# Adding the experts' rows to the residual by scatters with addition instead of gathering them in a closing stage

## What is computed

```
h   = h + moe(rmsnorm(h, ffn_norm))
# moe: each row picks one of 4 groups and 2 of the 4 experts in it; 16 experts, FF = 256
for e in range(16):
    he = silu(t @ w1[e]) * (t @ w3[e])
    y  = y + gates[:, e:e+1] * (he @ w2[e])
y_prompt, y_sample = rmsnorm(h[meta rows dropped], final_norm)
```

## Time and profile before

| | us |
|---|---|
| median of 3 runs (1346.1 to 1353.96) | 1346.58 |
| the profiled execution | 1341.16 |
| its span, first to last instruction | 1339.4 |
| busy in the span: PE / DVE / ACT / POOL | 1141.3 / 718.1 / 506.5 / 310.0 |

### The profile page before, as it was taken

One profiled execution on the slowest core, in us unless ns is written; L12 is line 12 of the kernel. 1 busy time (PEld: TensorE's weight loads), 2 busy tenths in 40 slices (PEclk: granted clock), 3 DMA queues, 4 the chain that ended last, 5 costly groups with the idle time before them and its releaser, 6 DMA issues.

```text
span 1339.4 us, 18555 instructions
## 1 busy us (share of the span) xinstructions
PE 1141.3 (85%) x5999; PEld 926.0 (69%) x5999; DVE 718.1 (54%) x1328; ACT 506.5 (38%) x909; POOL 310.0 (23%) x274
## 2 busy tenths in 40 slices
PE   4999999989898989989899999965988989899800
PEld 3888899934776777777787776854776767777600
DVE  3430510155645554545454553447777777788646
ACT  3334221133212222122223232305767777777611
POOL 2100400000000000000000000004665666666454
PEclk9999999999878988898999999976999999999965
DMA  6340141180101011110101010006778876673287
GB/s 241 108 146 0 56 131 50 48 252 19 32 17 52 32 64 37 43 63 17 63 17 63 17 48 9 32 32 199 266 263 277 277 271 230 240 246 130 79 324 256
DMA packets 93987, 158.93 MB, mean 119 GB/s; under 512 B 13712, under 2 KB 62304, under 8 KB 93920
## 3 DMA queue, kind: packets, MB, share of 16 engines
q1 hardware_dynamic: 81152, 113.49, 25.0%
q0 software_dynamic: 11680, 42.47, 9.2%
q10 hardware_dynamic: 1088, 2.10, 0.4%
HBM read 167.81 MB, written 40.55 MB: 156 GB/s over the span
## 4 chain that ended last, share of the span: by engine, by line
PE 57%; DVE 12%; DMA 10%; issue 9%; ACT 6%; SPq 2%; POOL 2%; POOLq 0%; ACTq 0%; DVEq 0%
PE ps L918 10%; DMA below<-in_w 7%; PE ps L885 5%; PE ps L755 4%; PE ps L773 4%; DVE low L1603 4%; PE ps L1926 4%; PE ps L1928 4%; PE ps L1927 4%; PE ps L844 3%; PE ps L1921 2%; PE ps L1920 2%; PE ps L1922 2%; SPq L1211 2%; ACT high L1318 2%
## 5 line engine op out<-in xcount | busy, mean ns | idle before, releaser
L1603 DVE TENSOR_TENSOR low<-below,high 128x1024 fp32r<-128x1024 f32 x128 | 198.2, 1595 | 70.0 <-ACT high L1318 62.6
L1784 POOL TENSOR_SCALAR arena<-arena 128x1 f32<-128x1 f32 (+5 forms) x38 | 14.8, 390 | 728.4 <-ACT arena L743 325.9
L1279 POOL TENSOR_TENSOR low<-below,high 128x1024 fp32r<-128x1024 f32 x64 | 148.5, 2340 | 106.3 <-ACT high L1339 106.3
L1416 PE MATMUL ps<-high 128*128 128x512 f32 x384 | 158.5, 413 | 16.1 <-DVE low L1613 11.4
L1418 PE MATMUL ps<-high,low 128*128 128x512 f32 x384 | 152.9, 398 | 0.0
L1417 PE MATMUL ps<-low,high 128*128 128x512 f32 x384 | 152.7, 398 | 0.0
L1318 ACT ACTIVATE high<-below 128x1024 fp32r<-128x1024 f32 x128 | 128.9, 1052 | 44.9 <-DMA below<-in_w 44.9
L553 ACT ACTIVATE arena<-ps 128x512 f32<-128x512 f32 (+7 forms) x109 | 56.9, 531 | 232.0 <-PE ps L755 231.6
L918 PE MATMUL ps<-arena 128*128 128x256 f32 (+1 forms) x576 | 133.3, 385 | 3.3 <-ACT arena L553 2.8
L918 PEld LDWEIGHTS ps<-arena 128*128 128x128 f32 (+1 forms) x576 | 107.1, 188 | 29.3 <-issue 6.7
L755 PE MATMUL ps<-arena 128*128 128x128 f32 (+4 forms) x613 | 100.3, 290 | 7.0 <-ACT arena L735 2.5
(11 more groups left out here) (215 smaller groups left out, 1988.4 us busy)
## 6 DMA issues: line engine op xcount, KB each, us to landing
below<-in_w SPq DMA_DIRECT2D x256, 256.0 KB
below<-in_w POOLq DMA_DIRECT2D x64, 512.0 KB
y_dram<-arena SPq DMA_DIRECT2D x32, 512.0 KB, 3.0
arena<-in_x_prompt SPq DMA_DIRECT2D x16, 512.0 KB
below<-in_w_in SPq DMA_DIRECT2D x12, 512.0 KB, 6.8
out<-arena SPq DMA_DIRECT2D x9, 512.0 KB, 6.7
arena<-in_w_o SPq DMA_DIRECT2D x1, 4096.0 KB, 16.6
h_dram<-arena SPq DMA_DIRECT2D x8, 512.0 KB, 2.6
```

The costliest lines, as they stand in the source:

```text
L1279: pool.tensor_tensor(w2_lo[s % UN][:, c], w2_in[:, c], w2_hi[s % UN][:, c].bitcast(F32), ALU.subtract).then_inc(s_w2lo, 1)
L1416: pe.matmul(out, x_hi, w_hi, start=start, stop=False)
L1603: dve.tensor_tensor(chunk(w13_lo[j], c), chunk(w13_in, c), chunk(w13_hi[j], c).bitcast(F32), ALU.subtract).then_inc(s_w13lo, 1)
```

## The change

The expert rows are no longer stored in `y_dram` and gathered. Instead POOL adds the 128 rows of each slot straight to the residual rows in `h1_dram` by an indirect DMA with addition, one after the other: two slots may hold the same row, so each waits for the landing of the one before. An empty place must not add to row 0; it is sent to one of 128 spare rows behind the T real ones, each place to its own. The spare rows are filled once by a DRAM to DRAM copy in the attention phase.

The gate has to be in the row before it is added, so it is multiplied into the gated product. For that a gate and a row number are needed for each place of a slot: `slot_gate` and `row_i`. They come from a second product on PE with `pos_at`: its other side, `more_at`, holds an indicator of occupied places and the gate in three bfloat16 parts, so that their sum is the float32 gate.

The closing stage loads all nine tiles of sums, squares, scales and stores them from the same buffer.

```diff
     # routing, after the gates
+        left = gates.rearrange("p k t -> p (k t)")
+        for n in range(3):
+            link(dve.tensor_copy(gate_part[:, n, :], left))
+            if n < 2:
+                link(dve.tensor_tensor(gate_rest[:, n, :], left, gate_part[:, n, :], ALU.subtract))
+                left = gate_rest[:, n, :]
...
-        dve.tensor_copy(slot_i, slot.rearrange("p (k t) -> p k t", k=2)).then_inc(s_slots, 1)
...
     # PE, between the product for tok_i and the turn of slot 0
+        pe.wait_ge(s_more, 4)
+        for k in range(2):
+            for t in range(NT):
+                n = k * NT + t
+                ins = pe.matmul(ps[:, 5, 0:4 * SLOT_TILES], pos_at[0:MOE_ROWS[t], n, :], more_at[0:MOE_ROWS[t], n, :],
+                                start=n == 0, stop=n == 2 * NT - 1)
+        ins.then_inc(s_moreps, 1)
...
     # DVE, before the loop
         split_weights(0, 0)
+        dve.tensor_copy(more_at[:, :, 0:SLOT_TILES], is_tile).then_inc(s_more, 1)
+        for n in range(3):
+            dve.tensor_tensor(more_at[:, :, (n + 1) * SLOT_TILES:(n + 2) * SLOT_TILES], is_tile,
+                              gate_part[:, n, :].unsqueeze(2).to_broadcast([P, 2 * NT, SLOT_TILES]),
+                              ALU.mult).then_inc(s_more, 1)
         dve.wait_ge(s_mx, 1)
         turned(0)
+        dve.wait_ge(s_moreps, 1)
+        held, far = ps[:, 5, 0:SLOT_TILES], row_f[:, 2, :]
+        dve.tensor_reduce(slot_gate, ps[:, 5, SLOT_TILES:4 * SLOT_TILES].rearrange("p (k s) -> p s k", k=3), AX.X, ALU.add)
+        link(dve.tensor_scalar(row_f[:, 0, :], held, -1.0, 1.0, ALU.mult, ALU.add))
+        link(dve.tensor_scalar(far, row_f[:, 0, :], tab[:, C_TOK:C_TOK + 1], float(T), ALU.mult, ALU.add))
+        link(dve.tensor_tensor(row_f[:, 1, :], far, row_f[:, 0, :], ALU.mult))
+        link(dve.tensor_tensor(row_f[:, 1, :], row_f[:, 1, :], rt[:, 23, 0:SLOT_TILES], ALU.add))
+        dve.tensor_copy(row_i, row_f[:, 1, :]).then_inc(s_rowi, 1)
...
     # DVE, in every slot
+            link_gate(s, j)      # gate_now[:, j] = slot_gate[:, s], then a wait for it
-            dve.tensor_tensor(g_row, act_h, ps[:, 3 + j, FF:2 * FF], ALU.mult).then_inc(s_mg, 1)
+            dve.scalar_tensor_tensor(out=g_row, in0=act_h, scalar=gate_now[:, j:j + 1], in1=ps[:, 3 + j, FF:2 * FF],
+                                     op0=ALU.mult, op1=ALU.mult).then_inc(s_mg, 1)
...
     # SP: no stores of y in the loop and none after it
     # SP, attention phase
+        sp.dma_start(h1_dram[T:T + P, :], x_prompt[0, 0:P, :]).then_inc(s_spare, 16)
     # POOL
+        def scatter(s):
+            if s == 0:
+                pool.wait_ge(s_rowi, 1)
+                pool.wait_ge(s_h1st, 16 * NT)
+                pool.wait_ge(s_spare, 16)
+            else:
+                pool.wait_ge(s_yst[(s - 1) % UN], 16 * ((s - 1) // UN + 1))
+            pool.wait_ge(s_mya, s + 1)
+            pool.wait_ge(s_myv, s + 1)
+            pool.indirect_dma_start(
+                out=h1_dram, out_offset=bass.IndirectOffsetOnAxis(ap=row_i[:, s:s + 1], axis=0),
+                in_=y_row[:, s % UN, :], in_offset=None, compute_op=ALU.add).then_inc(s_yst[s % UN], 16)
...
             if s + UN < SLOT_TILES:
                 gather(s + UN)
+            if s >= 2:
+                scatter(s - 2)
+        for s in range(SLOT_TILES - 2, SLOT_TILES):
+            scatter(s)
...
     # closing stage, SP
+        for j in range(UN):
+            sp.wait_ge(s_yst[j], 16 * uses(j))
         for t in range(NT):
             R = MOE_ROWS[t]
+            sp.dma_start(res[0:R, t, :], h1_dram[t * P:t * P + R, :]).then_inc(s_res[t], 16)
     # POOL: no fetch, rsqrt_mean alone. ACT squares res[t] when it has landed. DVE, for each tile:
+            dve.scalar_tensor_tensor(out=x, in0=x, scalar=y_stat[0:R, 1, t:t + 1], in1=fin_b[0:R, :], op0=ALU.mult,
+                                     op1=ALU.mult).then_inc(s_yo, 1)
```

More of the change, by code:

```diff
@@ L245, in hybrid_layer @@
     gates = r.take(2, NT)
-    slot_i = r.take(2, NT).bitcast(I32)
+    row_i = r.take(SLOT_TILES).bitcast(I32)
+    slot_gate = r.take(SLOT_TILES)
+    gate_now = r.take(2)
     tok_i = r.take(SLOT_TILES).bitcast(I32)
@@ L252, in hybrid_layer @@
     spread = Region(r.at)
-    is_tile = spread.take(2 * NT, SLOT_TILES)
     spread.at = (spread.at + 1) // 2 * 2
     tok_at = spread.take(2 * NT, SLOT_TILES).bitcast(BF16)
-    pos_at = spread.take(2 * NT, P // 2).bitcast(BF16)
     at_least = spread.take(2 * NT, SLOT_TILES)
@@ L270, in hybrid_layer @@
     (xg_hi, xg_lo), (g_hi, g_lo) = ([q.take(*dims) for q in (hi, lo)] for dims in ((KC, P), (2, P)))
-    r = Region(keep.at + 8000)
[L273 to L277, removed]
+    late = Region(below_floats + hi.at)
+    is_tile = late.take(2 * NT, SLOT_TILES)
+    pos_at = late.take(2 * NT, P // 2).bitcast(BF16)
+    more_at = late.take(2 * NT, 2 * SLOT_TILES).bitcast(BF16)
+    gate_rest = late.take(2, 2 * NT)
+    gate_part = late.take(3, NT).bitcast(BF16)
+    row_f = late.take(3, SLOT_TILES)
+    assert late.at <= below_floats + parts_floats
+    r = Region(keep.at + 8000)
+    res = r.take(NT, D)
     fin_b = r.take(D)
@@ L280, in hybrid_layer @@
     y_stat = r.take(2, NT)
-    h1_dram = nc.dram_tensor("h1_dram", [T, D], F32).ap()
+    h1_dram = nc.dram_tensor("h1_dram", [T + P, D], F32).ap()
     hn_dram = nc.dram_tensor("hn_dram", [T, D], F32).ap()
@@ L287, in hybrid_layer @@
     f_dram = nc.dram_tensor("f_dram", [P, HH, T], F32).ap()
-    y_dram = nc.dram_tensor("y_dram", [SLOTS, D], F32).ap()
     phase_end = sem("phase_end")
@@ L1126, in hybrid_layer @@
     s_rank = sem("s_rank")
-    s_slots = sem("s_slots")
+    s_spare = sem("s_spare")
+    s_gate = sem("s_gate")
+    s_more = sem("s_more")
+    s_moreps = sem("s_moreps")
+    s_rowi = sem("s_rowi")
     s_etab = sem("s_etab")
@@ L1153, in hybrid_layer @@
     s_fin_w = sem("s_fin_w")
-    s_res = [sem(f"s_res{i}") for i in range(FB)]
-    s_yab = [sem(f"s_yab{i}") for i in range(FB)]
-    s_comb = sem("s_comb")
+    s_res = [sem(f"s_res{i}") for i in range(NT)]
     s_ysq = sem("s_ysq")
@@ L1159, in hybrid_layer @@
     s_yo = sem("s_yo")
-    s_yout = [sem(f"s_yout{i}") for i in range(FB)]
+    s_yout = sem("s_yout")
     UN = 2
@@ L1212, in body @@
                                  cond=new).then_inc(s_w13in[c], 16)
[L1213 to L1220, removed]
         expert_turns(sp, body)
-        for s in range(SLOT_TILES - 3, SLOT_TILES):
-            store_y(s)
-            sp.dma_start(y_dram[s * P:(s + 1) * P, :], y_row[:, s % UN, :]).then_inc(s_yst[s % UN], 16)
         sp.wait_ge(phase_end, 12)
         sp.dma_start(fin_b, final_norm.rearrange("(a n) -> a n", a=1).to_broadcast([P, D])).then_inc(s_fin_w, 16)
[L1230 to L1238, removed]
+        for j in range(UN):
+            sp.wait_ge(s_yst[j], 16 * uses(j))
         for t in range(NT):
             R = MOE_ROWS[t]
+            sp.dma_start(res[0:R, t, :], h1_dram[t * P:t * P + R, :]).then_inc(s_res[t], 16)
+        for t in range(NT):
             sp.wait_ge(s_yo, t + 1)
             if t < 8:
-                sp.dma_start(y_prompt[0, t * P:(t + 1) * P, :], y_out[:, t % FB, :]).then_inc(s_yout[t % FB], 16)
+                sp.dma_start(y_prompt[0, t * P:(t + 1) * P, :], res[:, t, :]).then_inc(s_yout, 16)
             else:
[L1245 to L1249, removed]
+                sp.dma_start(y_sample[0], res[0:SAMPLE, t, :]).then_inc(s_yout, 16)
+        sp.wait_ge(s_yout, 16 * NT)
     def moe_pool(pool, rsqrt_mean):
@@ L1303, in moe_pool @@
             rsqrt_mean(y_stat[0:R, 1, t:t + 1], y_stat[0:R, 0, t:t + 1], D, s_ysq, s_yrs, t + 1)
-            if t + FB < NT:
-                fetch(t + FB)
     def moe_act(act):
@@ L1375, in moe_act @@
             R = MOE_ROWS[t]
-            act.wait_ge(s_comb, t + 1)
+            act.wait_ge(s_res[t], 16)
             if t:
                 act.wait_ge(s_ysq, t)
-            act.activation(y_sq[0:R], res[0:R, t % FB, :], ACT.Square,
+            act.activation(y_sq[0:R], res[0:R, t, :], ACT.Square,
                            accum_out=y_stat[0:R, 0, t:t + 1]).then_inc(s_ysq, 1)
@@ L1620, in moe_dve, with link_gate @@
         split_weights(0, 0)
+        dve.tensor_copy(more_at[:, :, 0:SLOT_TILES], is_tile).then_inc(s_more, 1)
[3 more added lines that the diff above has]
+                              ALU.mult).then_inc(s_more, 1)
         dve.wait_ge(s_mx, 1)
         turned(0)
+        dve.wait_ge(s_moreps, 1)
[6 more added lines that the diff above has]
+        dve.tensor_copy(row_i, row_f[:, 1, :]).then_inc(s_rowi, 1)
+        def link_gate(s, j):
+            dve.tensor_copy(gate_now[:, j:j + 1], slot_gate[:, bass.ds(s, 1)]).then_inc(s_gate, 1)
+            dve.wait_ge(s_gate, s + 1)
         def body(it, j, first, last):
@@ L1652, in moe_dve @@
         dve.wait_ge(s_fin_w, 16)
-        def finish(t):
+        for t in range(NT):
             R = MOE_ROWS[t]
```

(3 more changed lines are left out.)

## The result

| | before | after |
|---|---|---|
| median, us | 1347.15 (1346.1 to 1353.96) | 1362.32 (1360.43 to 1371.1) |
| profiled execution | 1341.16 | 1360.43 |
| its span | 1339.4 | 1358.7 |

The ratio is 1.012, 95% interval 1.0084 to 1.0155: the changed kernel is slower by 1.2%. Two later rounds on other chips gave 1.0145 (1.0106 to 1.0184) and 1.0113 (1.0072 to 1.0155). The forecast was 1353.6; its own range was 1340 to 1360, and the range over all rivals 1326 to 1382.

A forecast was written before the change was run, and what follows sets the result against it. Bound: a DVE-PE-ACT ring per slot, DMA slightly late for new experts, and a byte-moving closing stage. Terms -25 +4 +4 +24 = +7 us gave 1348 profiled, 1353.6 median; range 1340 to 1360, with rivals 1326 to 1382.

The forecast's parts named there:

- The sum: Whole change: -25 closing stage, +4 start, +4 gate copy, +24 scatters in the loop, together +7 us.
- the three stretches: Router's first operation to first turn of rows, loop to last y copy, closing stage: forecast +4, +28 and -25 us.
- Part 1: Closing stage: gathers, multiply-adds and y_dram traffic go, three serial scatters and nine loads remain; 25 us gained, bounds 7 to 34.
- the cadence: Closing stage: time per tile at the slowest station for the eight tiles after the first, taken as 2.1 us.
- Part 2: Start, before the first turn of rows: more gate operations and PE's second routing product delay it, +4 us, bounds 1 and 6.
- the linked operations: Start, ahead of the routing: five more gate operations in a chain, +1.0 us, minus 0.1 for a removed copy.
- Part 3: Loop, DVE: the gate copy before the gated product adds 0.2 us per turn, +4 us in all, bounds 2.5 and 10.
- the ring: Loop, slot with its expert loaded: DVE splits, gated product, PE turn, ACT splits, DVE's next splits; period 10.61 us.
- Part 4: Loop: scatter traffic beside the last weight chunks costs 1.6 us per new expert, 15 times, +24 us, bounds 5 and 38.
- A: Rival, loop: scatter traffic hides in idle DMA time, load term 0 to 6 instead of 24, 1330 to 1336 us; chance 0.3.
- B: Rival, loop: scatter landings over 10.6 us set the period; at 12 us +43, total 1382 us; chance 0.13.
- C: Rival, loop: weight loads lose the full double price, 2.5 us each, +38 instead of 24, 1368 us; chance 0.22.

The follow-up runs named there:

- the repaired kernel: Changed kernel with gate copied a slot ahead, gate parts and second product after the first turn, no POOL drain, roots in five groups: 1348.75 us, ratio to before 1.0016.
- plain scatters: Changed kernel with scatters that overwrite full rows instead of adding: 1351.31 us, ratio to before 1.0016.
- thin ones: Changed kernel with scatters that do not add and write only the first 64 of 1024 columns, to a narrow tensor of their own: 1327.42 us, one execution.
- b_store_mid: Kernel before, with SP's store of y of slot s-3 moved from after the fourth weight chunk to after the second: 1357.09 us, ratio 1.0072.
- after_again: The changed kernel once more, unchanged, on another chip: 1366.73 us, ratio to before 1.0145.

## Why the prediction came out as it did

**Sign and size.** The sum was +7 on the three stretches and they gave +10.2; the time is 8.7 us over the forecast, 2.3 over its own range of 1340 to 1360 and inside the wide one. Within 1% was held likelier (0.38) than slower (0.34); it came out just beyond. The good sum is in part luck: the closing stage gave 4.5 us less than forecast and the loop grew by 2.1 less.

**Part 1, closing stage, -25 forecast, -20.5 measured.** L (a scatter's time from issue to landing) was taken as 6, and the last ones follow each other at 6.1 to 6.3; scatter 29 was put 8.4 us ahead of y 31's arrival and came 8.5; the cadence was taken as 2.1 and is 2.00, with POOL's operation at 1.28 us beside DVE's. The term that failed is one that is not in the sum: POOL's drain. It was read from nothing, because in before it lay hidden behind the last slots, and it held the loads back 4.3 us, shown by the repaired kernel. The first load also landed in 5.3 us instead of 4.1.

**Part 2, start, +4 forecast, +4.8 measured.** From the router's first operation to DVE's weight splits it is 1.3 us longer, where 0.9 were forecast for the linked operations; the product took 2.44 us instead of 2.0. Moving the gate parts and the product out of the way brought 26.1 back, which shows that this stretch was all theirs.

**Part 3, gate, +4 forecast.** 0.2 us in the ring was 0.18 and another 0.07 for the product, which had been put at 0. Shown are five free slots instead of eight, 1.3 us; in the slots with loads the term stays open.

**Part 4, scatters, +24 forecast, 21.7 measured** (after less the kernel without them, one execution each), 1.4 per new expert against 1.6. The mechanism is the one forecast, traffic beside the last weight chunk. The chunks on the chain between 957 and 1215 us took 5.0 to 8.6 us in before, 9.1 to 12.3 in after, 8.6 to 10.0 with plain scatters, 5.1 to 8.4 without scatters and 5.4 to 8.0 with thin ones, and the loop is long or short with them. POOL's issues and the waits for landings are excluded as causes; bytes and packets were not parted. The working was right for a partly wrong reason: it took its bounds from the addition (1.3 us plain, 2.5 double) and chose low. In fact plain scatters already cost about 16 us (20 against the thin ones), 1.1 to 1.4 per expert and so the full plain price, and the addition, though it about doubles a row's engine time, adds 0.4 to 0.9 each.

**The rule on the shared engines.** The Trainium skill (DMA: Bandwidth & Descriptors, Issuing engines are not separate DMA queues) says that transfers from all issuing engines run on the same 16 DMA engines and interleave. This case's runs agree: plain scatters from POOL's queue made SP's weight chunks land later, 8.6 to 10.0 us against 5.1 to 8.4 without them. Stores behind the weights in SP's own queue cost nothing that can be read: the loop of before is 356.5 us with them, and the loops without full rows of y are 360.7 and 356.3.

**The rivals.** A (it hides) is refuted: ACT's wait for weights rose from 29.1 to 32.0 us to between 47.6 and 53.2, as the forecast had it (some 50). B (the landing becomes the ring) is too: landings were 5.8, 8.0 and at most 10.9 us under periods of 10.8 and more, and POOL waited for them 1.0 us in the whole loop. C would have needed 2.5 per expert.

**What stays open.** The medians differ by 15 to 19 us, the three stretches by 10.2. In the profiles the rest lies ahead of the router, whose first operation came at 892.7 us in before, at 908.3 and 909.8 in the two other profiles of before's attention phase (the second with the copy added), and between 899.1 and 907.2 in the ten of the others. The copy of the spare rows is not the cause, neither by its presence nor by its place. The clock accounts for an estimated 10 us here: only the profile of before had the upper level between 342 and 362 us, and that execution, 1341.16, is 6 us below the median of before. With before's own attention phase b_store_mid reached the router later than after did, so this part goes with the execution and not with the change. Why the medians are still 5 to 9 us further apart than the stretches is not shown; the differences between loops, up to 7 us, may be part of it.

## What to carry to other kernels

Before a store is moved to another queue, ask what it stood behind: here a transfer that cost nothing behind a critical load cost its full time beside it, and its traffic mattered, not the instruction that issued it. A store put ahead of loads in one queue can do harm in another way, by making the queue wait for what is to be stored; look at the issuing engine's waits before you blame the bytes. A serial chain with waits for landings can be priced well from gathers of the same size; look also for a drain that today is hidden behind other engines. Anything put on the ring of a loop, however small, is paid in every turn that the ring sets, and may be done a turn ahead.

## What the runs showed of the hardware that I had not expected

**The clock fell after a wait of 3 us.** PE waited 3.00 us for the gated product of a slot whose last weights were late, and the matmuls after it took 0.63 us instead of 0.39. Timeline and windows of after (clock is the figure ahead of the last two):

```profile
1149.93 0.39 PE L1413 MATMUL ps<-high,low 128*128 128x512 f32 x1
1153.32 0.44 PE L1469 MATMUL ps<-arena 128*128 128x128 f32 x2 [3.00 <-DVE arena L1651]
...
1155.20 0.63 PE L1413 MATMUL ps<-high,low 128*128 128x512 f32 x1
...
1150.00:1153.30 3.30, 0.32 (x2) 0.00 (x0) 1.97 (x5) 2.79 (x5) 2.71 (x2) 1.00 0.98 344
1154.20:1157.60 3.40, 3.39 (x8) 2.72 (x9) 1.75 (x4) 3.40 (x4) 2.39 (x2) 0.50 0.84 160
```

The granted clock was 1.00 (2.4 GHz) up to 1153.3 and 0.50 (1.2 GHz) over the 3.4 us after the wait. In stretches of 3 us there are nine such falls in the loop of after behind its first 12 us, and three in that of before. Over the loop the clock went from 0.97 to 0.94, and PE was busy 8.8 us longer for the same matmuls. How much of that stands on the path was not separated; in after_again PE was busy 4.4 us less than in after (clock 0.96), and the loop was as long.

**A row of 4 KB takes 382 ns of a DMA engine when it is added and 177 when it overwrites**, by the estimate above. The whole adding scatter of 512 KB lands in 5.8 us at best and 8.0 in the median, the overwriting one in 3.3 and 5.0. **POOL's drain** ended about 10 us after the last scatter's issue, some 4 us after the landing on which the repaired kernel lets the loads go.
